# A two-layer decoder trunk on one core: block sums begun in the pooling stage of layer 0; norm weights, operand sums and the first weight pair of layer 1 in another order

## The reference

```python
for l in range(2):
    h = rms_norm(x, norm_gains[l, 0])
    z = h @ w_in[l]                                   # 768 main + 256 memory features
    y_main = pool_mixer(...) if l == 0 else dilated_mixer(...)
    y_mem = memory_attn(z_mem, mem, ...)
    y = concatenate([y_main, y_mem]) @ w_out[l]
    x = x + rms_norm(y, norm_gains[l, 1])
    h = rms_norm(x, norm_gains[l, 2])
    gu = h @ w_gate_up[l]
    y = (silu(gu[:, :2816]) * gu[:, 2816:]) @ w_down[l]
    x = x + rms_norm(y, norm_gains[l, 3])
    if l == 0:
        shared = build_shared_kv(x, ...)
```

## Time and profile before

| | us |
|---|---|
| median of 3 runs | 2199.73 |
| lowest, highest | 2196.04, 2201.51 |
| the profiled execution | 2191.11 |
| its span, first to last instruction | 2189.3 |
| PE busy | 2082.3 |
| DVE busy | 1470.6 |
| ACT busy | 955.4 |
| POOL busy | 339.9 |
| mean granted clock of TensorE | 0.981 |

### The profile page before, as it was taken

How to read it: one execution, slowest core, us unless ns; L and a number is a source line. 1 busy time by engine, 2 the same in 40 slices (tenths; PEclk the granted TensorE clock), 3 DMA queues, 4 the chain that set the end, 5 groups by cost and what they waited for, 6 DMA issues and landing times.

```text
span 2189.3 us, 25430 instructions
## 1 busy us (share of the span) xinstructions
PE 2082.3 (95%) x9458; PEld 1678.2 (77%) x9458; DVE 1470.6 (67%) x2079; ACT 955.4 (44%) x1513; POOL 339.9 (16%) x188
## 2 busy tenths in 40 slices
PE   8998489999999999999999998999989999999997
PEld 6776378888888888887777776678778888887886
DVE  5556477567788775675455466577779999885565
ACT  5335144355554454343445556664622222234441
POOL 3633000012121000000000023020023333310001
PEclk9999789999999999999999999999999999999998
DMA  4204762255678876574111100113236654477554
GB/s 168 92 15 174 263 224 92 87 202 216 218 276 295 302 282 231 186 289 162 58 59 58 58 30 30 39 54 121 77 103 245 240 191 173 173 263 253 191 188 153
DMA packets 119755, 357.37 MB, mean 163 GB/s; under 512 B 10832, under 2 KB 12112, under 8 KB 114384
## 3 DMA queue, kind: packets, MB, share of 16 engines
q1 hardware_dynamic: 103168, 325.59, 42.0%
q10 hardware_dynamic: 16464, 30.15, 4.0%
HBM read 241.28 MB, written 114.43 MB: 162 GB/s over the span
## 4 chain that ended last, share of the span: by engine, by line
PE 72%; DVE 9%; DMA 8%; ACT 5%; issue 5%; SPq 1%; POOL 0%; ACTq 0%; POOLq 0%; DVEq 0%
PE PS L941 10%; PE PS L943 10%; PE PS L942 10%; PE PS L716 7%; PE PS L721 6%; PE PS L717 6%; PE PS L959 5%; PE PS L960 5%; PE PS L961 5%; PE PSC L865 3%; DMA s_keep<-ZS 2%; PE PO L837 2%; DMA TP<-x_mid 1%; PE PTR L847 1%; DMA ZS<-in_wdn 1%
## 5 line engine op out<-in xcount | busy, mean ns | idle before, releaser
L959 PE MATMUL PS<-RP,DH 128*128 128x512 f32 x616 | 241.4, 392 | 3.0 <-DVE RP L2165 3.0
L960 PE MATMUL PS<-RP,DH 128*128 128x512 f32 x616 | 240.3, 390 | 0.0
L961 PE MATMUL PS<-RP,DL 128*128 128x512 f32 x616 | 240.2, 390 | 0.0
L941 PE MATMUL PS<-BHT,SH 128*128 128x512 f32 x576 | 224.1, 389 | 0.0
L942 PE MATMUL PS<-BLT,SH 128*128 128x512 f32 x576 | 224.1, 389 | 0.0
L943 PE MATMUL PS<-BHT,SL 128*128 128x512 f32 x576 | 224.1, 389 | 0.0
L941 PE MATMUL PS<-BH,SH 128*128 128x512 f32 x432 | 168.3, 390 | 3.9 <-DVE TP L2004 3.1
L942 PE MATMUL PS<-BL,SH 128*128 128x512 f32 x432 | 168.1, 389 | 0.0
L943 PE MATMUL PS<-BH,SL 128*128 128x512 f32 x432 | 168.1, 389 | 0.0
L959 PEld LDWEIGHTS PS<-RP,DH 128*128 128x128 f32 x616 | 116.0, 188 | 28.4 <-DVE RP L2165 4.3
L1076 ACT ACTIVATE DH<-DR 128x1408 fp32r<-128x1408 f32 x56 | 77.3, 1380 | 132.5 <-DMA DR<-s_keep 85.6
(11 more groups left out here) (327 smaller groups left out, 4828.7 us busy)
## 6 DMA issues: line engine op xcount, KB each, us to landing
SR<-in_wst SPq DMA_DIRECT2D x36, 1024.0 KB, 4.9
ZS<-in_wdn SPq DMA_DIRECT2D x32, 704.0 KB, 5.9
s_keep<-ZS SPq DMA_DIRECT2D x32, 704.0 KB, 4.7
DR<-s_keep SPq DMA_DIRECT2D x32, 704.0 KB, 5.0
WR<-in_w SPq DMA_DIRECT2D x36, 512.0 KB, 4.3
inner<-TP SPq DMA_DIRECT2D x36, 512.0 KB, 4.3
DR<-in_wdn SPq DMA_DIRECT2D x24, 704.0 KB, 5.5
RR<-t_keep SPq DMA_DIRECT2D x16, 1024.0 KB, 5.2
```

The source lines that it names most:

```text
L941: MM(BANK[bank], SH[b][:, w, c], BH[t][:, k, :], start=(k == 0), stop=False)
L959: MM(bank, wh[:, i, :], rh, start=(i == 0), stop=False)
L960: MM(bank, wh[:, i, :], rl, start=False, stop=False)
L961: ins = MM(bank, wl[:, i, :], rh, start=False, stop=(i == KD - 1))
```

## The change

Layer 0: SP issues the first four output weights, then the first two blocks; the other four weights are issued after the load of block 4. DVE makes the sums of block 0 in the pooling stage before and between the two steps of pooling job 1, in two halves, and those of blocks 1 and 2 after the steps of jobs 3 and 4; blocks 3 to 7 follow in the first five turns of the output projection.

Layer 1: ACT multiplies the norm weight into half 0 while it waits for that half's norm, and into half 1 inside the residual loop, two tiles behind. `t_make(1, 0)` waits for 12 multiplied tiles instead of 16; two operand sums stand before the gate of (0, 1) and two behind. Splits, gates and low parts are ordered anew, and the first pair's load is issued before the first product of half 1 is kept, and its high part before gate (2, 1). In layer 0 the order of these steps stays as it was.

```diff
@@ ACT, sub_layer(1)
                     weight_hi(ffn[4])
+                    for k in range(3):
+                        scale_x(0, k)
                     norm_root(s_x, 0)
+                    for k in range(3, 7):
+                        scale_x(0, k)
                     norm_row(s_x, 0)
+                    scale_x(0, 7)
                     weight_hi(ffn[5])
...
-                    for k in range(4):
+                    for k in range(KT):
                         residual(r, 1, k)
-                    gate(l, 2, 0)
-                    for k in range(4, KT):
-                        residual(r, 1, k)
+                        if k > 1:
+                            scale_x(1, k - 2)
+                        if k == 3:
+                            gate(l, 2, 0)
                     gate(l, 3, 0)
-                    scale_x(0, 0)
-                    scale_x(0, 1)
+                    scale_x(1, 6)
                     norm_root(s_x, 1)
-                    for k in range(2, 6):
-                        scale_x(0, k)
+                    scale_x(1, 7)
                     norm_row(s_x, 1)
-                    for k in (6, 7):
-                        scale_x(0, k)
-                    for k in range(KT):
-                        scale_x(1, k)
                 q0 = NPAIR * l
-                gate(l, 0, 1)
-                for q in range(3):
-                    t_split(l, q)
-                gate(l, 1, 1)
+                if l == 0:
+                    gate(l, 0, 1)
+                t_split(l, 0)
+                t_split(l, 1)
+                if l:
+                    gate(l, 0, 1)
+                t_split(l, 2)
+                if l == 0:
+                    gate(l, 1, 1)
                 t_split(l, 3)
+                if l:
+                    gate(l, 1, 1)
+                    st_raw_hi(q0)
                 gate(l, 2, 1)
-                st_raw_hi(q0)
+                if l == 0:
+                    st_raw_hi(q0)
                 st_sum_hi(q0)
@@ DVE, pooling stage
+            def weight_sums(l, c, part=None):
+
+                z = block_buffer(l, c)
+                if part != 1:
+                    dve.wait_ge(*sums_seen(l, c))
+                    link(V.tensor_tensor(z[:, 3, :], z[:, 2, :], z[:, 3, :], ALU.add))
+                    link(V.tensor_tensor(z[:, 2, :], z[:, 0, :], z[:, 2, :], ALU.subtract))
+                if part != 0:
+                    link(V.tensor_tensor(z[:, 0, :], z[:, 3, :], z[:, 0, :], ALU.subtract))
+                    V.tensor_tensor(z[:, 1, :], z[:, 1, :], z[:, 0, :], ALU.subtract).then_inc(sums_made, 1)
...
             for n, m in enumerate(POOL_OUT):
-                step()
-                step()
+                for part in range(2):
+                    if n == 1:
+                        normalise(att["DVE"] - 1)
+                        weight_sums(0, 0, part)
+                    step()
                 if n == 1:
                     pooled_tile(5)
                 if n == 5:
                     step()
+                if n in (3, 4):
+                    weight_sums(0, n - 2)
@@ DVE, t_make
-                    dve.wait_ge(x_scaled, 2 * KT)
+                    dve.wait_ge(x_scaled, 2 * KT if q else KT + 4)
@@ DVE, sub_layer(0)
                         accumulate(s_y, 0, m)
-                        weight_sums(0, m)
+                        if m < 5:
+                            weight_sums(0, m + 3)
@@ DVE, sub_layer
                     invert(s_x, 1)
+                q0 = NPAIR * l
+                t_make(l, 0)
+                t_make(l, 1)
+                if l:
                     gate_scaled(0, 1)
-                q0 = NPAIR * l
-                for q in range(4):
-                    t_make(l, q)
+                t_make(l, 2)
+                t_make(l, 3)
                 t_low(l, 0)
                 product(l, 0, 1)
                 t_low(l, 1)
-                t_low(l, 2)
                 if l:
                     gate_scaled(1, 1)
+                t_low(l, 2)
                 t_low(l, 3)
@@ SP, sub_layer
                 if l == 0:
-                    loads_to(J[("ffn", 0, (0, 0), 0)])
+                    loads_to(J[("out", 0, 4, 0)])
                     sp.wait_ge(mm_done, J[("in", 0, POOL_IN[-1], None)] + 1)
                     load_blocks(0, 0)
                     load_blocks(0, 1)
...
                         keep_blocks(0, c)
                         if c + 2 < 8:
                             load_blocks(0, c + 2)
+                        if c == 2:
+                            loads_to(J[("ffn", 0, (0, 0), 0)])
...
                     keep_half(l, f, 0)
+                load_pair(l, NHT)
                 keep_half(l, 0, 1)
-                load_pair(l, NHT)
                 keep_half(l, 1, 1)
```

More of the change, by code:

```diff
@@ L2134, in pair_product @@
                 V.tensor_tensor(PRD[q % 2], G[:, :], UP[:, :], ALU.mult).then_inc(st_prod, 1)
[L2136 to L2143, removed]
             def inner_sums(l, f):
```

## The result

The changed kernel took 2175.68 us (median of 5 runs, 2174.77 to 2183.56), the kernel before 2197.65 us beside it (5 runs, 2195.51 to 2201.51): ratio 0.9904, 95% interval [0.9883, 0.9925]. The prediction was 2186.7 us, range 2179 to 2197. The direction was right and the time missed by 11 us, 3.3 us outside the range. The profiled execution took 2175.9 us (span 2174.1, granted clock 0.986) against 2191.11 before, 15.2 us less where 13 had been worked out. The larger part of the miss therefore lies between the profiled execution of before and its other runs.

The account below looks back on a forecast made before the run. PE, busy 95% of the span, bounds the kernel, so only its waits can be gained: -8 in layer 0 and -5 in layer 1 take 2191.11 to 2178.1, and 8.6 to the median gives 2186.7 us (range 2179 to 2197).

Parts of the forecast that it names:

- Block 0's stall: Layer 0 pooling: DVE waits for block 0 from 162 to 177, PE stops, projection starts 18 us later.
- The ring gives the stall back: Layer 0 projection: the earlier chain of block loads, sums and keeps returns PE to full flow at 278, not 285.8.
- late output weights: Layer 0 projection: output weights 4 to 7, queued behind block 4's load, arrive just in time and cost nothing.
- Rival 3: Layer 0 pooling: block 0 lands at 190 or later, making the kernel slower; 2206.7 at a landing of 197; chance 0.06.
- Part B: Layer 1: new orders and an earlier pair load remove PE's waits at products and first pair; gain 5 us.
- eighth scaling: Layer 1, first half: ACT's last norm-weight multiplication, behind the row, is the only one exposed; costs 0.65 us.
- waits of 2.6 and 3.1 us: Layer 1: PE's waits for two products (2.6) and before the first weight pair (3.1), both claimed to go.
- early load: Layer 1: first pair's load ahead of keep_half(0, 1) goes at 1587.5 and readies the pair's weights before PE needs them.
- A: Layer 0: block sums 0 to 2 moved into the pooling stage; net gain 8 us, between -12 and -3.
- term of +8.6: Whole run: profiled execution before lay 8.6 us under the runs' median; the same difference was added to 2178.1.
- Rival 1: Layer 0 pooling: short stall, block 0 lands at 173, shift 14, sum -17; 2182.7 us, chance 0.14.
- Rivals 2, 3 and 4: Layer 0: 2, stall spreads, 2191.7 to 2193.7, chance 0.15; 3, slower, 0.06; 4, pooling-stage sums give nothing, 2194.7, 0.10.

Follow-up runs that it names:

- blocks first: Changed kernel with blocks 0 and 1 loaded ahead of the last two pooling weights and first four output weights; 2161.39 us, ratio 0.9849 to before.
- late-sums kernel: Changed kernel with sums of block 0 behind the fourth pooling tile, block 1 behind the fifth, block 2 behind the attention loop; 2172.34 us, ratio 0.9897.
- layer-1 part: Kernel before plus layer 1's new orders and the first pair's load ahead of the keep in both layers; 2190.13 us, ratio 0.9976.
- part A alone: Kernel before plus only the layer-0 edits to block sums and load queue, layer 1 and pair loads as before; 2182.04 us, ratio 0.9942.
- block 7 late: Changed kernel with block 7's sums behind DVE's reciprocal for the norm, not ahead of the last three square accumulations; 2172.02 us, ratio 0.9891.
- pair order: Changed kernel with layer 0's first pair load put back behind keep_half(0, 1), layer 1 keeping its new order; 2177.37 us, ratio 0.9914.
- block 1 early: Changed kernel with block 1's sums behind the steps of the third pooling tile instead of the fourth's; 2175.85 us, ratio 0.9900.

## Why the prediction was right and wrong

**Block 0's stall: right.** Worked out were a landing at 177, a DVE wait from 162, a shift of 18. Measured: 178.07 with 16.16 us of wait, and 18.4. The clock in the stall was 0.68, and one sum of block 1 beside a GpSimd instruction took 3.08 us for 0.89.

**The ring gives the stall back: right in kind, small by 3 us.** The prediction had block 3's keep landed at 237 and block 7's sums done at 270.3. SP's row at 234.29, which waits for that keep, and the sums' end at 267.5 (263.80 and four sums of 0.9) show 3 us less. Full flow came at 274.85, not at 278: **-10.9 where -8 was worked out**. The ring's first load went out 28.2 us earlier (196.24 to 168.07), the ring ran 10.7 us longer (85.0 to 95.7), and the last block came 17.4 us earlier (281.20 to 263.80). It ran longer because DVE's order, and not the transfers, set the sums of blocks 1 to 4.

The prediction's rule, 1 us of return for each us of shift, holds where the sums keep their places: blocks first shifts the projection by 2.6 us instead of 18.4 and is in full flow at 259.09, 15.8 us earlier for a shift 15.8 smaller. It fails in the late-sums kernel, with a shift of 6.0 and full flow at 275.82. The prediction put the late output weights at nothing, with the remark that a lost cover costs 1 us for each us. In the changed kernel the cover just held (DVE waited 0.27 us); in the late-sums kernel it was gone (8.92). Rival 3 did not come about, since block 0 landed at 178; its price, one for one with the landing, is not tested.

**The move in layer 0: missed.** The text costed the pair's load ahead of the keep in layer 1 alone. The same lines run in layer 0, where the margin is smaller: +1.4 us, shown by its presence in the layer-1 part (1.28 us at 408.32) and in the changed kernel and its absence with the order put back. From a later row of PE that waits for SS (344.29 in the changed kernel) to the first pair, the six kernels with this wait take 64.95 to 65.19 us, the eight without it 63.35 to 63.42: 1.5 to 1.8 us.

**Part B: right in total, wrong in one reason.** Predicted -5.0; the layer-1 part alone measured -5.3. The eighth scaling cost 0.5 (0.65 said), the waits of 2.6 and 3.1 us went, the BL waits stayed. Wrong: the early load gives nothing, and keep_half(0, 1) behind it, issued at 1577.45, let DVE go on at 1585.65, 8.2 us later, where 2.5 had been worked out (DVE waited 3.63 us); PE's queue of work hid it. In the two profiled executions the pair starts 15.8 us earlier, more than A and B explain: the granted clock in 1560 to 1580 was 0.83 before and 1.00 after, worth 3.4 us. In four other profiles of unchanged or half-changed kernels it was 0.74, 0.83, 0.91 and 0.94. Kernels with the whole of layer 1's new order settle whose it is. In 1545 to 1565, where the changed kernel has 1.00, late sums and block 7 late have 0.83, pair order and block 1 early 0.91. So it belongs to the execution and not to the change.

The differences to before along PE's rows, in us, add up:

| place (before) | difference | what came in |
|---|---|---|
| 285.8 | -10.9 | ring |
| 438.7 | -9.5 | product wait +1.4 |
| 1463.0 | -7.0 | granted clock in 1400 to 1420: 1.00 before, 0.83 after |
| 1560.4 | -6.5 | eighth scaling +0.5 |
| 1614.5 | -15.8 | waits -5.7, clock -3.4 |
| 1995.3 | -13.5 | PE's waits for RP in 1945 to 1982 |
| 2174.8 | -15.0 | granted clock in 1990 to 2010: 0.91 before, 1.00 after |

**The step that failed: from one execution to the median.** The prediction added 8.6 us, the distance of the profiled execution of before from the median of three runs, to the changed kernel. The changed kernel's profiled run (2175.9) lies 0.2 us above its median: the term of +8.6 measured -0.2. Of the 11.0 us of miss, 8.8 are this step. The other 2.2 lie in the profiled execution, where the ring, the product wait and layer 1 (-10.9 + 1.4 - 5.2 = -14.7) are the change and the rest is the clock and small waits of one execution. The distance was not a constant tax: the profile of before was a fast execution (2191.11; of the 22 runs beside the first set only three lie below it and their median is 2194.5, and the unchanged kernel's next profile took 2197.62), and 4 us of it sat in the SS wait (29.1 against 33.2 to 33.4) that the change cuts. Against the 288.7 to 289.9 at which the other three profiles of this ring have full flow, part A alone (276.35) is worth 12.4 to 13.5 us, and its runs say 12.7. A term that an edit removes must be taken at its typical size. Another 2 to 5 us come from the three runs of before shown, whose median (2199.73) lay above that of the five beside the changed kernel (2197.65) and of the 22 (2194.5).

Rival 1, 2182.7, came nearest in time and for the wrong reason: the shift was 18.4, not 14. Rivals 2, 3 and 4 are out by the traces.

## What to carry to other kernels

When an edit makes an engine wait earlier in a chain of loads and stores, don't add up the stall: find which link releases the next one. Here it was the place of block 2's sums in DVE's order, with the output weights queued behind block 4's load: moving sums without moving the queue gained nothing, and issuing two loads 14 us earlier, which also ended the stall, gained 14. Work that only frees a buffer should not stand ahead of the last accumulation that the other engine waits for. And a loop body that serves both layers must be costed in both.

## What the runs showed of the hardware

The same ring took 85.0 us in one execution and 87.2 to 87.3 in three others of the old queue, and 92.8 to 100.1 in the new. The transfers at its end were not slower: the last keep ahead of the last load took 9.16 us after and 9.24 before, the last load 7.21 and 7.22. More moved at once while the output weights were inserted (329 GB/s in 216 to 245 after, 255 in 204 to 245 before).

A block sum takes 0.89 us on DVE. In all 14 profiles each one of layer 0 that took over 1.5 us, up to 3.10, overlapped an instruction of GpSimd; in the changed kernel this met four of the 32 (at 200.24, 223.53, 231.09 and 234.20). A few others overlapped one as well and stayed at 0.89, so the overlap is shown and its mechanism is not.

The projection stage with the ring varied by several us between profiles of nearly the same code. The next one, bound by PE, did not: from that later row of PE to the first pair's product it took 63.35 to 63.42 us in the eight kernels without the product wait (349.11 to 412.48 in the pair-order run).

Taking a long idle away from TensorE also changed its clock. Before, it had 0.54 in 245 to 274, half of full speed or 1.2 GHz for nearly all of it; after, 0.88. With block 7's sums late it had 1.00 there:

```profile
245.00:274.00 29.00, 29.00 (x136) 24.09 (x135) 17.82 (x23) 8.21 (x14) 0.81 (x1) 1.00 0.79 272
```
